# Differences of weight quarters written over the quarters themselves, and seven quarter products for the keys and values of a cross-attention

## The chip, the cores and the metric

The kernel runs on one core of a Trainium2 chip. The time is that of the whole kernel on the device, in microseconds (us). A single profiled execution gives the trace; its span runs from the first to the last instruction.

## The reference, cut to what matters

One layer works on `x` (256 tokens of 2048). The memory `mem` has 256 tokens of 2048 too. All is fp32. The parts that the change touches are the output projection behind the mixing stage and the memory's keys and values:

```python
h = h + jnp.concatenate([y_r, y_a], axis=-1) @ w_out[l]     # (256, 2048) @ (2048, 2048)
mem_n = rms_norm(mem, mem_norm[l])
k = (mem_n @ wk).reshape(B, M, XATT_HEADS, XATT_HEAD_DIM)    # (256, 2048) @ (2048, 512)
v = (mem_n @ wv).reshape(B, M, XATT_HEADS, XATT_HEAD_DIM)    # (256, 2048) @ (2048, 512)
s = jnp.einsum('bthd,bmhd->bhtm', q, k) * (XATT_HEAD_DIM ** -0.5)
```

Ahead of the projection stands an RWKV-7 recurrence over eight pairs of heads (`y_r`) beside a windowed attention (`y_a`). Behind the cross-attention stands a mixture of 32 experts, of which each has three matrices of 4 MB.

## The kernel before, in words

**Stages, in order of time.** The input projection runs to some 365 us. The recurrence then takes its eight pairs of heads one after the other, each some 26 us (the function `pair_`, once in the program of every engine). Then come the output projection in four blocks of 512 output columns, the memory's keys and values, the queries, scores and values of the cross-attention, the router, and the experts, from some 850 us to the end.

**Inside a pair.** TensorE runs 24 small steps (L1932 to L1967), each let go by a copy of ScalarE (L779, L781) and, for the last eight, by a sum that GpSimd makes with the identity (L539). VectorE meanwhile masks, scales and norms. At its start a pair adds an identity on GpSimd (L533) and sums keys (L536). What follows the 24 steps is L1973 to L2035 on TensorE, with VectorE at L1269 to L1287.

**A block of the output projection.** It is a product of 256 x 2048 by 2048 x 512, both cut in quarters: A11, A12, A21, A22 are 128 tokens by 1024, and B11, B12, B21, B22 are 1024 by 256. Seven products of sums of quarters replace eight of the quarters. Product number i stands in PSUM bank i; it is eight steps of 128 rows of the weights, and every fp32 step of 256 columns is two TensorE instructions in the trace. So a block has 56 steps, or 112 instructions (L2064). The sums of the left side (S1 to S4) are made during the recurrence by GpSimd (L544 to L549), those of the last head pair by VectorE (L1346 to L1351). The differences of the right side are T1 = B12 - B11, T2 = B22 - T1, T3 = B22 - B12 and T4 = B21 - T2, each one VectorE instruction of 128 x 2048. T1, T2 and T4 stand in the first 24 KB of `rest`, T3 over B12. Those of block 0 are made in the last pair (L1202 to L1218, called in `pair_` under `if last:`); those of block n + 1 are made while block n is multiplied.

VectorE collects the products with `w_op` and `w_add` (L1353 to L1366), 12 instructions in a block. Each of them waits for the one before it through the semaphore `op_add`, and for the product through `op_mm`.

**Between the last pair and block 0.** The last head pair's norm is still to be made: a mean on TensorE (L2056), the deviation and its square on VectorE (L1164, L1165), the variance on TensorE (L2076), the inverse root on ScalarE (L731, L733), and then VectorE to `gated` (L1181) and the last sums. The first 30 steps of block 0 (seven of product 1, eight of products 2 and 4, seven of product 5) need nothing of that result.

**Keys and values before.** `features` (L2111) makes keys turned over, features by tokens: four groups of 16 steps of 256 columns, 64 steps or 128 instructions. The values are 32 steps of 512 columns, 64 instructions (L2125). ScalarE copies each result out (L812, L815). `turn` (L1688) transposes a norm's rows on TensorE, 32 instructions; `turned` copies them back, half on VectorE and half on ScalarE.

**Weight loads.** The ring has three slots of 4 MB. `where` gives the slot of each load; SP issues each one when its slot's user before it has signalled `used`. Behind the values SP starts the experts' stream (`gate_up(0, "wg", 0)`), and from there each load waits for a step of TensorE.

## Time and profile before

| | us |
|---|---|
| median of three runs | 1792.4 (1790.73 to 1794.39) |
| the profiled execution | 1793.52 |
| its span | 1791.7 |
| TensorE matmul busy | 1692.2 (94%) |
| VectorE busy | 618.9 (35%) |
| ScalarE busy | 338.2 (19%) |
| GpSimd busy | 124.7 (7%) |

The profiled execution lies 1.1 us above the median, and its span 1.8 us under its own time. A timeline row gives the start, the duration of the whole merged group, the engine, the line and operation, the tiles, the number of instructions, and in brackets how long the engine had been idle and what ended that. The duration of a merged group runs from the first start to the last end; the next group may start before that end, since matmuls are pipelined. A source line can be that of a helper: all products stand at L2064, all collecting instructions at L1357. "issue" is a wait of an engine for which the profile shows no releaser.

### The profile page before, as it was taken

Reading aid. Unit: us, or ns where it says so; the run is one execution under the profiler, and the core shown is the slowest. Engines: PE = TensorE matmul, PEld = TensorE weight load, DVE = VectorE, ACT = ScalarE, POOL = GpSimd, SP = SyncE. Lnnn points to the kernel's source line nnn. Section 1 sums busy time; section 2 is a strip of 40 time slices with the busy share of each in tenths; the row PEclk is TensorE's granted clock in tenths of the full one; section 3 lists DMA queues with packets and bytes.
Section 4 is the critical chain, followed back from the end, with each engine's and each line's share of the span. In section 5 each row is a group of like instructions: output and inputs, shape, how many; then the busy total and the mean of one; then the engine's idle time right before and its main releaser. Section 6 shows DMA issues by size and latency. Waiting matters only on the chain.

```text
span 1791.7 us, 36478 instructions
## 1 busy us (share of the span) xinstructions
PE 1692.2 (94%) x15655; PEld 1123.0 (63%) x15655; DVE 618.9 (35%) x1330; ACT 338.2 (19%) x966; POOL 124.7 (7%) x206
## 2 busy tenths in 40 slices
PE   8999999989998999999999999999999999999996
PEld 7887888877777888576554554445444545454543
DVE  2001333488887462023123222232223222322233
ACT  2112222157666101122000000000000000000002
POOL 1000000013235000001000000000000000000000
PEclk9999999999999999999999999999999999999999
DMA  9932434300000944436999999999999999999995
GB/s 304 220 113 94 121 118 175 110 3 4 4 4 4 338 169 158 186 157 242 415 393 425 432 427 434 426 434 429 430 429 432 430 429 430 430 432 424 409 421 208
DMA packets 100783, 503.59 MB, mean 281 GB/s; under 512 B 38204, under 2 KB 42704, under 8 KB 81472
## 3 DMA queue, kind: packets, MB, share of 16 engines
q1 hardware_dynamic: 95960, 489.22, 68.2%
q0 software_dynamic: 4464, 12.03, 2.3%
q8 instruction: 94, 1.54, 0.4%
q10 hardware_dynamic: 248, 0.65, 0.1%
q14 instruction: 17, 0.14, 0.0%
HBM read 511.29 MB, written 4.23 MB: 288 GB/s over the span
## 4 chain that ended last, share of the span: by engine, by line
PE 70%; DMA 21%; DVE 4%; issue 2%; SPq 1%; ACT 1%; POOL 1%; DVEq 0%; ACTq 0%; POOLq 0%
PE ps L1734 15%; DMA rest<-in_wd 9%; DMA ring<-in_wu 9%; PE ps L2288 8%; PE ps L2280 8%; PE ps L2431 8%; PE ps L2064 5%; PE ps L2296 4%; DMA rest<-in_wu 2%; PE ps L2116 2%; PE ps L2167 2%; PE ps L2184 2%; PE ps L2125 2%; DMA ring<-in_wg 1%; PE ps L1951 1%
## 5 line engine op out<-in xcount | busy, mean ns | idle before, releaser
L1734 PE MATMUL ps<-wide,ring 128*128 128x256 f32 x1248 | 275.3, 379 | 1.2 <-PE ps L1734 0.9
L1734 PEld LDWEIGHTS ps<-wide,ring 128*128 128x128 f32 x1248 | 239.0, 195 | 39.7 <-issue 10.1
L2288 PE MATMUL ps<-ring,wide 128*64 128x256 f32 x1472 | 170.8, 391 | 28.9 <-DMA ring<-in_wu 28.7
L1594 DVE TENSOR_TENSOR tokA<-tokA,ps 128x512 f32<-128x512 f32 x256 | 158.5, 682 | 102.1 <-PE ps L2296 102.1
L2280 PE MATMUL ps<-ring,wide 128*64 128x256 f32 x1600 | 178.8, 381 | 2.9 <-DVE wide L1582 1.9
L1607 DVE SCALAR_TENSOR_TENSOR gg<-ps,tmp,gg 128x256 f32<-128x256 f32 x32 | 15.5, 484 | 472.4 <-PE ps L2288 472.4
L2431 PE MATMUL ps<-ring,gg 128*64 128x512 f32 x736 | 168.1, 598 | 0.8 <-DMA ring<-in_wd 0.8
L2288 PEld LDWEIGHTS ps<-ring,wide 128*64 128x64 f32 x1472 | 107.7, 141 | 91.3 <-DMA ring<-in_wu 36.9
L2280 PEld LDWEIGHTS ps<-ring,wide 128*64 128x64 f32 x1600 | 113.6, 137 | 60.2 <-DVE wide L1582 3.3
L2296 PE MATMUL ps<-wide,gg 64*128 64x512 f32 x512 | 135.3, 627 | 0.6 <-ACT wide L926 0.6
L2431 PEld LDWEIGHTS ps<-ring,gg 128*64 128x64 f32 x736 | 48.7, 136 | 114.5 <-issue 106.9
L918 ACT ACTIVATE wide<-ps 128x512 f32<-128x512 f32 x32 | 19.1, 598 | 449.7 <-PE ps L2431 449.7
L915 ACT ACTIVATE gg<-ps,tmp 128x256 f32<-128x256 f32 x32 | 15.2, 475 | 339.9 <-PE ps L2280 339.9
L570 POOL DMA_INDIRECT wide<-h_dram,sidx x17 | 17.1, 1008 | 889.9 <-DVE sidx L1546 889.1
L779 ACT ACTIVATE ring<-ps 128x384 f32<-128x384 f32 (+2 forms) x184 | 70.8, 421 | 27.9 <-PE ps L1954 7.5
L2296 PEld LDWEIGHTS ps<-wide,gg 64*128 64x128 f32 x512 | 41.5, 185 | 54.5 <-issue 50.2
L1013 DVE TENSOR_SCALAR tokA<-tmp,dprm 128x256 f32<-128x256 f32 x22 | 7.8, 354 | 192.3 <-ACT tmp L660 192.3
L2431 PE MATMUL ps<-rest,gg 128*64 128x512 f32 x288 | 65.5, 598 | 3.4 <-DMA rest<-in_wd 2.3
L2288 PE MATMUL ps<-rest,wide 128*64 128x256 f32 x528 | 58.8, 379 | 1.8 <-DMA rest<-in_wu 1.8
L2288 PEld LDWEIGHTS ps<-rest,wide 128*64 128x64 f32 x528 | 37.7, 137 | 21.6 <-DMA rest<-in_wu 3.0
L2280 PE MATMUL ps<-rest,wide 128*64 128x256 f32 x448 | 49.9, 381 | 0.0
L2431 PEld LDWEIGHTS ps<-rest,gg 128*64 128x64 f32 x288 | 19.8, 136 | 46.2 <-issue 39.2
(381 smaller groups left out, 2203.7 us busy)
## 6 DMA issues: line engine op xcount, KB each, us to landing
ring<-in_wu SPq DMA_DIRECT2D x20, 4096.0 KB, 29.5
ring<-in_wg SPq DMA_DIRECT2D x19, 4096.0 KB, 28.4
ring<-in_wd SPq DMA_DIRECT2D x19, 4096.0 KB, 30.8
rest<-in_wd SPq DMA_DIRECT2D x8, 4096.0 KB
ring<-in_w_in SPq DMA_DIRECT2D x7, 4096.0 KB, 16.4
rest<-in_wg SPq DMA_DIRECT2D x6, 4096.0 KB
rest<-in_wu SPq DMA_DIRECT2D x6, 4096.0 KB
ring<-in_w_out SPq DMA_DIRECT2D x4, 4096.0 KB, 19.5
```

Source lines behind the costliest of these rows:

```text
L779: ins = A(PRN[(l + 1) % 2][:, g, :, k], got[:, :, k], ACT.Copy)
L1594: V.tensor_tensor(fin_part(t, h, n), fin_part(t, h, n), ps[:, banks[q][h], :], ALU.add).then_inc(S["added"], 1)
L1734: ins = mm(ps[0:rows_, m % 2, 0:T], lhs, hnT[:, k, :], start=k == 0, stop=k == KD - 1)
L2064: ins = mm(ps[:, i, 0:T], lhs[:, k], rhs[:, k], start=k == 0, stop=k == CT - 1)
L2116: ins = mm(ps[:, f, 0:T], slot_k(s)[:, k, P * f:P * f + P], x[:, k, :], start=k == 0, stop=k == KD - 1)
L2125: ins = mm(ps[:, 4 + b, :], memT[:, k, P * b:P * b + P], slot_k(where[L_V])[:, k, :], start=k == 0, stop=k == KD - 1)
L2167: ins = mm(ps[:, f % 2, 0:T], slot_k(where[L_Q])[:, k, P * f:P * f + P], hnT[:, k, :], start=k == 0, stop=k == KD - 1)
L2184: ins = mm(ps[:, WO_BANK[n], :], oT[:, h, P * b:P * b + P], slot_d(where[L_O])[:, h, q], start=h == 0, stop=h == XH - 1)
L2280: ins = mm(ps[CAP * h:CAP * h + CAP, 0, 0:T], xT[:, k, CAP * i:CAP * i + CAP], in_k(p)[:, k, T * h:T * h + T], start=k == 0, stop=k == KD - 1)
L2288: ins = mm(ps[CAP * h:CAP * h + CAP, 1, 0:T], xT[:, k, CAP * i:CAP * i + CAP], w[:, T * h:T * h + T], start=k == 0, stop=k == KD - 1)
L2296: ins = mm(ps[:, banks[q][h], :], OHT[rows_, i, P * t:P * t + P], ysb[rows_, F * n:F * n + F], start=True, stop=True)
L2431: ins = mm(ps[CAP * h:CAP * h + CAP, 4 + n, :], half(hgT, k), in_d(dn)[:, k, o:o + F], start=k == 0, stop=k == 3)
```

## The change

The differences now stand in the quarters' own places: T1 over B11, T3 over B12, T2 over B22, T4 over B21. Each can be written only when the product of the quarter under it has been made, so they are made inside their own block; the products run in the order 1, 2, 3, 5, 7, 6, 4 (block 0: 2, 1, 3, 5, 7, 6, 4). None is made in the last pair. In block 0, T1 comes in two pieces, seven eighths behind the first seven steps of product 1 and one eighth behind its last. There the variance's matmul stands behind two steps of product 2; the steps ahead of the last pair's result are 22.

Keys and values become blocks 4 and 5 of the same kind, with the quarters of the turned memory on the left. Four sums of 128 x 1024 (M_S1 to M_S4) are made on VectorE behind the memory's turn. The collecting instructions are 8 in each of the two. Keys now come out tokens by features, so eight transposes on TensorE and two copies on ScalarE turn them, between products of the values. The norm of the cross-attention's rows (`normed(2)`) moves behind the keys' differences on VectorE.

```diff
@@ -207,8 +207,11 @@
-        W_T1, W_T2, W_T4 = (rest[:, CT * T * n:CT * T * n + CT * T].rearrange("p (k n) -> p k n", n=T) for n in range(3))
         W_U = tmp[:, 1280:1536]
+        M_A11, M_S3, M_A12, M_A22 = memT[:, 0:CT, 0:P], memT[:, 0:CT, P:T], memT[:, CT:KD, 0:P], memT[:, CT:KD, P:T]
+        M_S1, M_S2 = (rest[:, 24 * T + C * n:24 * T + C * n + C].rearrange("p (k t) -> p k t", t=P) for n in range(2))
+        M_S4 = oT[:].rearrange("p h t -> p (h t)").rearrange("p (k t) -> p k t", t=P)
+        krow = tmp[:, 0:1024].rearrange("p (b n) -> p b n", b=2)
...
@@ -282,6 +285,7 @@
+        W_BASE = (0, 12, 24, 36, 48, 56, 64)
...
@@ -807,15 +811,12 @@
             std(2, 3, "sq_done", 6)
-            for f in range(4):
-                act.wait_ge(S["xk_mm"], f + 1)
-                A(kxT[:, f, :], ps[:, f, 0:T], ACT.Copy).then_inc(S["xk_ev"], 1)
-            for b in range(TB):
-                act.wait_ge(S["xk_mm"], 5 + b)
-                A(vx[:, b, :], ps[:, 4 + b, :], ACT.Copy).then_inc(S["xk_ev"], 1)
+            for n in range(2):
+                act.wait_ge(S["xk_mm"], n + 1)
+                A(kxT[:, 2 * n:2 * n + 2, :].rearrange("p f t -> p (f t)"), ps[:, 0, :], ACT.Copy).then_inc(S["xk_ev"], 1)
...
-                    dve.wait_ge(S["op_mm"], 7 * (n - 1) + 4)
-                V.tensor_tensor(W_T1, W_B12(n), W_B11(n), ALU.subtract).then_inc(S["w_t"], 1)
...
-                V.tensor_tensor(W_T2, W_B22(n), W_T1, ALU.subtract).then_inc(S["w_t"], 1)
+            def w_t1(n, k=slice(0, CT)):
+
+                ins = V.tensor_tensor(W_B11(n)[:, k], W_B12(n)[:, k], W_B11(n)[:, k], ALU.subtract)
+                if k.stop == CT:
+                    ins.then_inc(S["w_t"], 1)
 
             def w_t3(n):
                 dve.wait_ge(*later("w_t", 4 * n + 1))
                 V.tensor_tensor(W_B12(n), W_B22(n), W_B12(n), ALU.subtract).then_inc(S["w_t"], 1)
 
+            def w_t2(n):
+                dve.wait_ge(*later("w_t", 4 * n + 2))
+                V.tensor_tensor(W_B22(n), W_B22(n), W_B11(n), ALU.subtract).then_inc(S["w_t"], 1)
+
...
+                dve.wait_ge(*later("w_t", 4 * n + 3))
+                V.tensor_tensor(W_B21(n), W_B21(n), W_B22(n), ALU.subtract).then_inc(S["w_t"], 1)
...
-                if last:
-                    w_t1(0)
-                    w_t2(0)
...
-                if last:
-                    w_t3(0)
-                    w_t4(0)
...
+            def made(n, count):
+                dve.wait_ge(S["op_mm"], 7 * n + count)
+
             w_ops = [0]
             dve.wait_ge(S["x2_in"], 16)
             for n in range(4):
+                dve.wait_ge(landed[where[L_OUT + n]], arrived[L_OUT + n])
                 if n == 0:
-                    dve.wait_ge(S["op_mm"], 1)
+                    made(n, 1)
                     w_add(n, 0, 0, product(2))
-                    dve.wait_ge(S["op_mm"], 2)
-                    w_add(n, 1, 0, product(4))
-                    dve.wait_ge(S["op_mm"], 3)
+                    dve.wait_ge(*later("w_p1", 1))
+                    w_t1(n, slice(0, CT - 1))
+                    made(n, 2)
                     w_op(W_U, product(1), None)
                     w_add(n, 0, 0, W_U)
...
+                    w_t1(n, slice(CT - 1, CT))
+                else:
+                    made(n, 1)
+                    w_op(W_U, product(1), None)
+                    w_add(n, 0, 0, W_U)
+                    w_t1(n)
+                    made(n, 2)
+                    w_add(n, 0, 0, product(2))
+                w_t3(n)
+                made(n, 3)
+                w_add(n, 0, 1, product(3))
+                w_t2(n)
+                w_t4(n)
+                made(n, 4)
+                w_add(n, 0, 1, product(5))
+                w_add(n, 1, 1, product(5))
+                made(n, 6)
...
+                made(n, 7)
                 w_add(n, 1, 0, product(4))
...
+            dve.wait_ge(S["hn_tr"], 16)
+            dve.wait_ge(S["hn_ev_a"], 8)
+            dve.wait_ge(S["hn_ev_v"], 8)
+            V.tensor_tensor(M_S1, M_S3, M_A22, ALU.add).then_inc(S["w_s7"], 1)
+            dve.wait_ge(*later("w_s7", 5))
+            V.tensor_tensor(M_S2, M_S1, M_A11, ALU.subtract).then_inc(S["w_s7"], 1)
+            dve.wait_ge(*later("w_s7", 6))
+            V.tensor_tensor(M_S4, M_A12, M_S2, ALU.subtract).then_inc(S["w_s7"], 1)
+            V.tensor_tensor(M_S3, M_A11, M_S3, ALU.subtract).then_inc(S["w_s7"], 1)
+
+            def memory_block(n, rows_):
+
+                lo, hi = slice(0, T), slice(T, 2 * T)
+                dve.wait_ge(landed[where[L_OUT + n]], arrived[L_OUT + n])
+                made(n, 1)
+                w_op(W_U, product(1), None)
+                w_t1(n)
+                made(n, 2)
+                w_op(rows_[:, 0, lo], W_U, product(2))
+                w_t3(n)
+                made(n, 3)
+                w_t2(n)
+                w_t4(n)
+                if n == 4:
+                    normed(2)
+                made(n, 6)
+                w_op(W_U, W_U, product(6))
+                w_op(rows_[:, 0, hi], W_U, product(5))
+                w_op(rows_[:, 0, hi], rows_[:, 0, hi], product(3))
+                w_op(W_U, W_U, product(7))
+                w_op(rows_[:, 1, hi], W_U, product(5))
+                made(n, 7)
+                w_op(rows_[:, 1, lo], W_U, product(4))
+
+            memory_block(4, krow)
+            memory_block(5, vx)
...
-            def product(n, i, lhs, rhs, ks=range(CT)):
-
-                if n >= 1 and ks[0] == 0:
-                    pe.wait_ge(S["op_add"], W_EACH * (n - 1) + (W_READ if n >= 2 else W_READ0)[i])
+            def product(n, i, lhs, rhs, ks=range(CT), ends=True):
...
-
-            W_READ0 = {2: 1, 4: 2, 1: 3, 5: 6, 6: 7, 3: 9, 7: 10}
-            W_READ = {1: 1, 2: 3, 6: 4, 5: 7, 7: 8, 3: 11, 4: 12}
+                return ins
+
+            W_READ0 = {2: 1, 1: 2, 3: 4, 5: 6, 6: 7, 7: 9, 4: 12}
+            W_READ = {1: 1, 2: 3, 3: 4, 5: 6, 6: 7, 7: 9, 4: 12}
+            M_READ = {1: 1, 2: 2, 6: 3, 3: 5, 7: 6, 5: 7, 4: 8}
             first, final = range(CT - 1), range(CT - 1, CT)
+
+            def combined_products(n, s1, s2, s3, a22):
+                pe.wait_ge(*later("w_t", 4 * n + 1))
+                product(n, 5, s1, W_B11(n))
+                pe.wait_ge(*later("w_t", 4 * n + 2))
+                product(n, 7, s3, W_B12(n))
+                pe.wait_ge(*later("w_t", 4 * n + 3))
+                product(n, 6, s2, W_B22(n))
+                pe.wait_ge(*later("w_t", 4 * n + 4))
+                product(n, 4, a22, W_B21(n))
+                pe.wait_ge(S["op_mm"], 7 * n + 7)
+                pe.sem_inc(used[where[L_OUT + n]], 1)
+
             landing(L_OUT)
-            pe.wait_ge(*later("w_t", 4))
-            pe.wait_ge(*later("w_s", 2 * (CT - 1)))
-            product(0, 1, W_A11, W_B11(0), first)
+            product(0, 2, W_A12, W_B21(0), range(0, 2))
             pe.wait_ge(S["rw_dsq"], CT)
             mm(ps[:, 7, T:2 * T], ones2, DSQ, start=True, stop=True).then_inc(S["rw_var"], 1)
-            product(0, 2, W_A12, W_B21(0))
-            product(0, 4, W_A22, W_T4)
-            product(0, 5, W_S1, W_T1, first)
+            product(0, 2, W_A12, W_B21(0), range(2, CT))
+            pe.wait_ge(*later("w_s", 2 * (CT - 1)))
+            product(0, 1, W_A11, W_B11(0), first).then_inc(S["w_p1"], 1)
+            product(0, 3, W_S4, W_B22(0), first)
             pe.wait_ge(S["rw_out"], CT)
             product(0, 1, W_A11, W_B11(0), final)
             pe.wait_ge(*later("w_s7", 4))
-            product(0, 5, W_S1, W_T1, final)
-            product(0, 6, W_S2, W_T2)
-            product(0, 3, W_S4, W_B22(0))
-            product(0, 7, W_S3, W_B12(0))
-            pe.wait_ge(S["op_mm"], 7)
-            pe.sem_inc(used[where[L_OUT]], 1)
+            product(0, 3, W_S4, W_B22(0), final)
+            combined_products(0, W_S1, W_S2, W_S3, W_A22)
             for n in range(1, 4):
                 landing(L_OUT + n)
                 product(n, 1, W_A11, W_B11(n))
                 product(n, 2, W_A12, W_B21(n))
-                pe.wait_ge(*later("w_t", 4 * n + 2))
-                product(n, 6, W_S2, W_T2)
-                product(n, 5, W_S1, W_T1)
-                pe.wait_ge(*later("w_t", 4 * n + 3))
-                product(n, 7, W_S3, W_B12(n))
                 product(n, 3, W_S4, W_B22(n))
-                pe.wait_ge(*later("w_t", 4 * n + 4))
-                product(n, 4, W_A22, W_T4)
-                pe.wait_ge(S["op_mm"], 7 * n + 7)
-                pe.sem_inc(used[where[L_OUT + n]], 1)
+                combined_products(n, W_S1, W_S2, W_S3, W_A22)
...
-            def features(n, x, count):
-                landing(n)
-                s = where[n]
-                for f in range(4):
-                    for k in range(KD):
-                        ins = mm(ps[:, f, 0:T], slot_k(s)[:, k, P * f:P * f + P], x[:, k, :], start=k == 0, stop=k == KD - 1)
-                    ins.then_inc(S["xk_mm"], 1)
-                pe.wait_ge(S["xk_mm"], count)
...
-            features(L_K, memT, 4)
+            def keys_turned(n):
+                for f in (2 * n, 2 * n + 1):
+                    for b in range(TB):
+                        o = T * (f % 2) + P * b
+                        ins = tr(ps[:, 0, o:o + P], krow[:, b, P * f:P * f + P], ident)
+                ins.then_inc(S["xk_mm"], 1)
+
+            landing(L_K)
+            product(4, 1, M_A11, W_B11(4))
+            product(4, 2, M_A12, W_B21(4))
+            pe.wait_ge(*later("w_s7", 8))
+            product(4, 3, M_S4, W_B22(4))
+            combined_products(4, M_S1, M_S2, M_S3, M_A22)
             landing(L_V)
-            for b in range(TB):
-                for k in range(KD):
-                    ins = mm(ps[:, 4 + b, :], memT[:, k, P * b:P * b + P], slot_k(where[L_V])[:, k, :], start=k == 0, stop=k == KD - 1)
-                ins.then_inc(S["xk_mm"], 1)
-            pe.wait_ge(S["xk_mm"], 6)
-            pe.sem_inc(used[where[L_V]], 1)
-            pe.wait_ge(S["xk_ev"], 6)
+            product(5, 1, M_A11, W_B11(5))
+            product(5, 2, M_A12, W_B21(5))
+            pe.wait_ge(S["op_add"], W_BASE[5])
+            keys_turned(0)
+            product(5, 3, M_S4, W_B22(5))
+            pe.wait_ge(S["xk_ev"], 1)
+            keys_turned(1)
+            combined_products(5, M_S1, M_S2, M_S3, M_A22)
+            pe.wait_ge(S["xk_ev"], 2)
+            pe.wait_ge(S["op_add"], W_BASE[6])
             pe.wait_ge(S["hn_done"], 3)
```

## Rows read from the trace of the kernel before

**Rows 1.** Chain of waits that ended last, shares of the span by engine, from the page.

```profile
PE 70%; DMA 21%; DVE 4%; issue 2%; SPq 1%; ACT 1%; POOL 1%; DVEq 0%; ACTq 0%; POOLq 0%
```

**Rows 2.** Busy time by stretch: us, each engine's busy us (instructions), TensorE's clock, DMA, GB/s.

```profile
579.80:584.70 4.90, 4.86 (x88) 3.58 (x89) 0.01 (x1) 2.93 (x10) 2.72 (x7) 0.65 0.02 3
...
590.50:616.10 25.60, 25.30 (x116) 21.96 (x116) 10.47 (x21) 5.35 (x8) 0.00 (x0) 1.00 1.03 397
...
1100.00:1791.00 691.00, 639.07 (x4346) 326.78 (x4342) 191.47 (x348) 58.31 (x156) 11.00 (x11) 0.99 0.97 414
```

**Rows 3.** Timeline (start, us, engine, line, idle before) of the last pair, several engines.

```profile
574.54 2.50 DVE L1212 TENSOR_TENSOR ring<-ring 128x2048 f32<-128x2048 f32 x1
...
575.13 0.44 PE L1964 MATMUL ps<-cst_sb,ring 128*128 128x128 f32 x2
...
575.60 5.23 POOL L539 TENSOR_TENSOR ring<-ring,cst_sb 128x128 f32<-128x128 f32 x5 [0.71 <-ACT ring L779]
...
576.96 2.50 DVE L1218 TENSOR_TENSOR rest<-ring,rest 128x2048 f32<-128x2048 f32 x1
...
579.78 1.21 PE L1957 MATMUL ps<-ring 64*64 64x64 f32 x24 [1.96 <-POOL ring L539]
...
584.69 0.29 DVE L1269 TENSOR_TENSOR ring<-ring,ps 128x128 f32<-128x128 f32 x1 [5.24 <-PE ps L1986]
```

**Rows 4.** Timeline of the same part of the pair before the last.

```profile
547.91 2.57 POOL L539 TENSOR_TENSOR ring<-ring,cst_sb 128x128 f32<-128x128 f32 x5 [7.63 <-ACT ring L779]
...
548.86 0.44 PE L1964 MATMUL ps<-cst_sb,ring 128*128 128x128 f32 x2
...
552.39 0.60 PE L1967 MATMUL ps<-tokA,cst_sb 128*128 128x256 f32 x2
...
552.92 0.34 PE L1957 MATMUL ps<-ring 64*64 64x64 f32 x8
...
555.12 0.29 DVE L1269 TENSOR_TENSOR ring<-ring,ps 128x128 f32<-128x128 f32 x1 [0.71 <-PE ps L1986]
```

**Rows 5.** Chain of waits in the last pair: start, us, what.

```profile
573.76 0.86 issue
```

**Rows 6.** Timeline from the end of the last pair into the first block, TensorE and VectorE.

```profile
590.53 0.70 PE L2056 MATMUL ps<-tmp,cst_sb 128*128 128x256 f32 x2 [0.94 <-DVE tmp L1287]
...
591.73 0.42 DVE L1165 TENSOR_TENSOR tmp<-tmp 128x256 f32<-128x256 f32 x1
...
594.09 0.59 PE L2076 MATMUL ps<-tmp,cst_sb 128*128 128x256 f32 x2
...
598.65 0.28 DVE L1351 TENSOR_TENSOR wide<-wide 128x128 f32<-128x128 f32 x1
```

**Rows 7.** Timeline at the end of the fourth block and the start of the turn.

```profile
686.37 3.62 PE L2064 MATMUL ps<-rest,wide 128*128 128x256 f32 x16
...
690.02 0.42 DVE L1357 TENSOR_TENSOR tokA<-tokA,ps 128x256 f32<-128x256 f32 x1 [3.03 <-PE ps L2064]
...
690.50 3.71 PE L1688 MATMUL ps<-cst_sb,rest 128*128 128x128 f32 x32 [0.52 <-DVE tokA L1357]
```

**Rows 8.** Groups by line and shape, 590 to 700 us: count, busy us, mean ns.

```profile
L1357 DVE TENSOR_TENSOR tokA<-tokA,ps 128x256 f32<-128x256 f32 x20 | 8.4, 420 | 21.4 <-PE ps L2064 21.1
...
L1212 DVE TENSOR_TENSOR ring<-ring 128x2048 f32<-128x2048 f32 x3 | 6.9, 2284 | 0.0
```

**Rows 9.** Timeline of the memory's keys and values and of the turn behind them.

```profile
695.14 27.89 PE L2116 MATMUL ps<-rest,ring 128*128 128x256 f32 x128 [0.93 <-ACT rest L642]
...
723.19 27.70 PE L2125 MATMUL ps<-ring,rest 128*128 128x512 f32 x64
...
751.58 3.71 PE L1688 MATMUL ps<-cst_sb,wide 128*128 128x128 f32 x32 [0.69 <-ACT rest L815]
```

**Rows 10.** Timeline of the DMA queue of SP: the expert stream's first load.

```profile
751.01 0.35 SPq L378 DMA_DIRECT2D ring<-in_wg  x1
```

**Rows 11.** Chain of waits, longest pieces: its first long wait for a weight load.

```profile
1101.49 30.15 DMA rest<-in_wu
```

More of the change, by code:

```diff
@@ L1196, in mask @@
                                 ps[:, 2 * g:2 * g + 2, 0:T].rearrange("p e (i n) -> p e i n", i=2), mk, ALU.mult).then_inc(S["rw_mask"], 1)
-            def w_t1(n):
-                dve.wait_ge(landed[where[L_OUT + n]], arrived[L_OUT + n])
-                if n >= 1:
-                    dve.wait_ge(S["op_mm"], 7 * (n - 1) + 4)
-                V.tensor_tensor(W_T1, W_B12(n), W_B11(n), ALU.subtract).then_inc(S["w_t"], 1)
-            def w_t2(n):
-                if n >= 1:
-                    dve.wait_ge(S["op_mm"], 7 * (n - 1) + (5 if n == 1 else 3))
-                dve.wait_ge(*later("w_t", 4 * n + 1))
-                V.tensor_tensor(W_T2, W_B22(n), W_T1, ALU.subtract).then_inc(S["w_t"], 1)
+            def w_t1(n, k=slice(0, CT)):
+                ins = V.tensor_tensor(W_B11(n)[:, k], W_B12(n)[:, k], W_B11(n)[:, k], ALU.subtract)
+                if k.stop == CT:
+                    ins.then_inc(S["w_t"], 1)
             def w_t3(n):
@@ L1212, in w_t3 @@
                 V.tensor_tensor(W_B12(n), W_B22(n), W_B12(n), ALU.subtract).then_inc(S["w_t"], 1)
+            def w_t2(n):
+                dve.wait_ge(*later("w_t", 4 * n + 2))
+                V.tensor_tensor(W_B22(n), W_B22(n), W_B11(n), ALU.subtract).then_inc(S["w_t"], 1)
             def w_t4(n):
-                if n >= 1:
-                    dve.wait_ge(S["op_mm"], 7 * (n - 1) + (2 if n == 1 else 7))
-                dve.wait_ge(*later("w_t", 4 * n + 2))
-                V.tensor_tensor(W_T4, W_B21(n), W_T2, ALU.subtract).then_inc(S["w_t"], 1)
+                dve.wait_ge(*later("w_t", 4 * n + 3))
+                V.tensor_tensor(W_B21(n), W_B21(n), W_B22(n), ALU.subtract).then_inc(S["w_t"], 1)
             def pair_(p, first, last, next_):
@@ L1377, in _ @@
                     w_op(W_U, product(1), None)
                     w_add(n, 0, 0, W_U)
-                    dve.wait_ge(S["op_mm"], 4)
-                    w_add(n, 0, 1, product(5))
-                    w_add(n, 1, 1, product(5))
-                    w_t1(n + 1)
-                    dve.wait_ge(S["op_mm"], 5)
-                    w_op(W_U, W_U, product(6))
-                    w_add(n, 0, 1, W_U)
-                    w_t2(n + 1)
-                    w_t3(n + 1)
-                    dve.wait_ge(S["op_mm"], 6)
@@ L1389, in _ @@
-                    w_add(n, 0, 1, product(3))
-                    dve.wait_ge(S["op_mm"], 7)
-                    w_op(W_U, W_U, product(7))
-                    w_add(n, 1, 0, W_U)
-                    w_add(n, 1, 1, W_U)
-                    w_t4(n + 1)
-                    continue
-                dve.wait_ge(S["op_mm"], 7 * n + 1)
-                w_op(W_U, product(1), None)
-                w_add(n, 0, 0, W_U)
-                dve.wait_ge(S["op_mm"], 7 * n + 2)
-                w_add(n, 0, 0, product(2))
@@ L1412, in _ @@
                 w_add(n, 1, 1, W_U)
-                if n < 3:
-                    w_t2(n + 1)
-                    w_t3(n + 1)
-                dve.wait_ge(S["op_mm"], 7 * n + 6)
-                w_add(n, 0, 1, product(3))
-                dve.wait_ge(S["op_mm"], 7 * n + 7)
+                made(n, 7)
                 w_add(n, 1, 0, product(4))
-                if n < 3:
-                    w_t4(n + 1)
                 if n == 1:
@@ L1424, in _ @@
             turned(1)
-            normed(2)
+            dve.wait_ge(S["hn_tr"], 16)
[31 more added lines that the diff above has]
+            memory_block(5, vx)
             turned(2)
@@ L2135, in scored @@
             def scored(h):
-                pe.wait_ge(S["xk_ev"], 7 + h)
+                pe.wait_ge(S["xk_ev"], 3 + h)
                 if h >= 2:
@@ L2174, in _ @@
                     valued(f - 3)
-            pe.wait_ge(S["xk_mm"], 10)
+            pe.wait_ge(S["xk_mm"], 6)
             pe.sem_inc(used[where[L_Q]], 1)
```

18 lines of the change are left out of this document (6 added, 12 removed).

## The prediction

> **What bounds the kernel now.** First the chain of waits from the page: TensorE carries 70% of it, weight loads 21%, VectorE 4% [rows 1]. Then the chain in order of time: its first long wait for a weight load comes at 1101 us [rows 11]. Ahead of that the end is set by TensorE and by who holds it up; behind it the DMA engines are busy for 97% of the time [rows 2]. All that the change touches lies between 565 and 752 us, in TensorE's part. The SP queue starts the experts' stream only at 751.01, when the values have let their slot go [rows 10], and each later load waits for a step of TensorE. So I take it that what TensorE gains before 751 moves the stream and the end with it, one for one.
>
> Last the timelines, for what each engine waits for. Three places count: the last pair, the start of block 0, and the keys and values.
>
> **The last pair: differences removed.** T3 and T4 of block 0 run on VectorE at 574.54 and 576.96, 2.5 us each. Beside them GpSimd takes 5.23 us for five small sums, and TensorE waits 1.96 us for one of them [rows 3]. In the pair before, the same five take 2.57 us [rows 4]. TensorE leaves that wait at a lower clock: 0.65 granted from 579.8 to 584.7, a mixture of 2.4 and 1.2 GHz [rows 2]. So the price is best read over the whole stretch. From the first transposes at L1964 to VectorE's first sum at L1269 the last pair needs 584.69 - 575.13 = 9.56 us [rows 3]. The pair before needs 555.12 - 548.86 = 6.26, of which 552.92 - 552.39 = 0.53 is the matmul at L1967, which the last pair hasn't [rows 4]; that leaves 5.73. **Gain: 9.56 - 5.73 = 3.8 us.** Lower bound: the wait that is seen, 1.96 [rows 3]. Upper bound: 3.8 and the 0.86 of "issue" just ahead [rows 5], 4.7, should that go too; nothing in the change speaks to it, and I leave it in. T1 and T2 lie beside GpSimd's key sums, which are wanted only behind the 24 steps, so I give their removal nothing.
>
> The Trainium skill, SBUF — State Buffer, section "SBUF: two separate sides", has a rule that bears on this: VectorE and GpSimd share a pair of ports, and a VectorE instruction with two SBUF inputs holds it whole while a GpSimd instruction that reads SBUF waits. The trace agrees: one wait of 1.96 us beside an instruction of 2.5 [rows 3]. By the rule alone only GpSimd's excess would come back, 5.23 - 2.57 = 2.7 us, and the forecast would be 1.1 us later.
>
> **The start of block 0.** A step of a product costs TensorE two instructions at (3.62 - 0.38) / 15 = 0.216 us, so 0.432 [rows 7]. From a product's last instruction to VectorE's start I take 690.02 - (686.37 + 16 x 0.216) = 0.19 us [rows 7]. I work in the clock of the old trace, without the shift from the pair.
> - The first product starts at 594.09 - 7 x 0.432 = 591.07 [rows 6]. Two steps on, at 591.93, the variance's matmul could go, but the squares are ready only at 591.73 + 0.42 = 592.15 [rows 6]: it goes at 592.2, a wait of 0.27, and 1.9 us earlier than now. The last sums of VectorE then end at 598.65 + 0.28 - 1.9 = 597.0 [rows 6].
> - TensorE goes on at 592.63 with 6 + 7 + 7 steps to 601.27, and two single steps to 602.13. Before, 30 steps stood here, and TensorE never waited.
> - VectorE needs 2.28 us for a difference of 2048 columns and 0.42 for 256 columns [rows 8], so some 2.0 for 1792. T1's long part starts when seven steps of product 1 are made, 592.63 + 13 x 0.432 + 0.19 = 598.4, and ends at 600.5. Product 1 is whole at 601.70 + 0.19 = 601.9; a copy, an add (0.42 each and a little between) and T1's rest then end at 603.1. Product 5 starts at 603.15.
> - New wait: 603.15 - 602.13 = 1.0 us. **Cost: 1.0 + 0.27 = 1.3 us.** Bounds: 0.3, if the collecting overlaps fully, and 2.5, if T1 cost in place by a half more.
> What is queued behind VectorE's waits in this block is only more collecting; nobody but TensorE waits for it.
>
> **The other differences, inside their blocks.** Nothing is added to VectorE's work, it is moved: 4 x 2.28 + 12 x 0.46 = 14.6 us in a block of 24.7. From a block's start: product 1 is there at 3.6, T1 at 6.9, wanted at 10.4; T3 at 9.8, wanted at 13.8; product 3 at 10.6, T2 at 13.3, wanted at 17.3; T4 at 15.6, wanted at 20.7. The shortest slack is 3.5 us, so **0** for blocks 1 to 3. One difference is already written in place, T3 over B12, at 2284 ns [rows 8]; the others should cost that. The last collecting instruction is still the add of product 4, so the turn starts as now, 0.06 behind it [rows 7]. `normed(1)` fits between blocks 1 and 2.
>
> **Keys and values.** Now keys take 723.19 - 695.14 = 28.05 us, of which 0.40 is handing over, and values 751.58 - 723.19 = 28.39, of which 0.9 is the end of the last matmul and ScalarE's copy [rows 9]. After:
> - Keys: 112 x 0.216 + 0.40 = 24.6.
> - Values: 24.2, eight transposes at (3.71 - 0.27) / 31 = 0.11 each [rows 9], 0.9, and at the end 0.19 + 0.42 + 0.06 for the last add, 0.7: 25.8.
> - **Gain: 56.4 - 50.4 = 6.0 us.**
> What must stay hidden: the four sums of 128 x 1024. Between the two durations of [rows 8], each is some 1.22 us, together 4.9 us from 695.1; product 3 wants them 6.9 us in. T1 of the keys then ends 8.0 us in, wanted at 10.4; T4 and `normed(2)` behind it end some 18.5 in, before product 6 is made at 20.9. The trace shows no such chain, so the bounds are 6.9 (no transposes in the way) and, if every sum waited in the open, 6.0 - 4.9 = 1.1. I take 6.0, since each link has a row. ScalarE's two copies of keys lie under products of 3.5 us. The rows' norm on VectorE is moved back by some 12 us and its turn is due 30 us later.
>
> **Sum.** -3.8 + 1.3 - 6.0 = -8.5 us. Against the profiled execution: 1793.5 - 8.5 = 1785.0, span 1783.2. That execution lay 1.1 above the median, so the median goes from 1792.4 to **1783.9**.
>
> **The rivals.**
> 1. *GpSimd is not freed* (0.12): something else holds the last pair, as code loading, of which the 0.86 of "issue" would be a part [rows 5]. Then the pair gives 0, and the sum is 1.3 - 6.0 = -4.7: 1787.7. Against it: the five sums are slow only in that pair [rows 3, 4].
> 2. *The clock falls at the new wait* (0.06). After 1.96 us of waiting the stretch behind ran at 0.65 for 4.9 us, which costs 4.9 x 0.35 = 1.7 us; after 0.94 us at 590.5 it stayed at 1.00 [rows 2, 3, 6]. The new wait is 1.0. If it fell: 1785.6. The Trainium skill, TensorE: Matmul & The Clock Gate, section "What's actually happening", says that the clock follows how busy TensorE has been of late; by that both rows fit, and the new wait is an open case.
> 3. *The memory's sums come into the open* (0.09): VectorE's chain behind the memory's turn is late, and the keys and values lose what they gain. -3.8 + 1.3 = -2.5: 1789.9.
> 4. *The loads swallow it* (0.08): the stream behind 1101 is bound by bytes, and if the transfers at 751 to 850 already ran against each other, an earlier start would bring little: some 1792. Against it: TensorE, not a load, carries the chain there [rows 11].
> 5. *Differences in place are dear* (0.05), the slow end. If VectorE took t for each when it writes what it reads, then from t = 3.9 us on T4 comes late by 4t - 15.7 in each of six blocks; from 4.3 us that eats the 8.5. At twice the row, 4.56: 6 x 2.5 + 1 = 16 lost, so 1792.4 - 8.5 + 16 = 1799.9. Against it: T3's row [rows 8].
>
> **How the numbers follow.** The forecast's own case has 0.60; with the bounds of its terms it runs from 1792.4 - 4.7 + 0.3 - 6.9 = 1781.1 to 1788. For the range I add what two executions differ by at the lower end, 1780.5, and reach up to rival 3, 1790.0. Outside are rivals 4 and 5 and a little of the rest. A measurement of this kernel can tell some 0.2%, 3.6 us, from no change. Faster than 1788.8: the forecast's case, rivals 1 and 2, and a part of 3: 0.80. Within: most of 3, and 4: 0.15. Slower: 0.05.
>
> **What the new profile would show.** GpSimd's last five sums at L539 in some 2.5 us and TensorE's clock at 1.00 behind them; L1964 to L1269 in 5.7 us. One wait of TensorE of 1.0 us before product 5 of block 0, on VectorE, and none in blocks 1 to 3. Keys' first product to the rows' turn in 50.4 us, against 56.4. SP's first load of the experts some 8.5 us earlier, at 742.5. It would be wrong if TensorE waited for VectorE ahead of products 3, 5, 7, 6 or 4 anywhere else, or if that load came 8.5 us earlier and the end did not.

## The result and the profile after

The changed kernel takes **1805.2 us** (median of four runs, 1804.0 to 1807.1) against 1792.8 for the kernel before (four runs too): a ratio of 1.0071, with an interval of 1.0053 to 1.0088. Faster by 8.5 us was forecast, in a range of 1780.5 to 1790.0; it is slower by 12.4 and lies 15 us above the range. The profiled execution took 1805.6, its span is 1803.8.

The chain of waits of the changed kernel, shares of the span by engine, and behind it the line of the page for the queue that loads program code (queue and kind, packets, MB, share of the DMA engines):

```profile
PE 89%; issue 4%; DVE 4%; ACT 1%; DMA 0%; POOL 0%; DVEq 0%; ACTq 0%
...
q8 instruction: 139, 2.28, 0.5%
```

Before, weight loads had 21% of this chain [rows 1]; now they have none. TensorE has 89% of it, and 4% is "issue". The kernel before had 94 code packets on queue 8:

```profile
q8 instruction: 94, 1.54, 0.4%
```

Turn 1 and turn 2 are the two passes of `turn` ahead of and behind the keys and values. Up to turn 2 the trace goes as forecast. This is the last pair after (timeline: start, us, engine, line, tiles, idle before). Its first row, L1976, is the transpose that stood at L1964 before; L543 are GpSimd's sums, at L539 before:

```profile
576.56 0.44 PE L1976 MATMUL ps<-cst_sb,ring 128*128 128x128 f32 x2
...
577.02 0.41 POOL L543 TENSOR_TENSOR ring<-ring,cst_sb 128x128 f32<-128x128 f32 x1 [0.78 <-ACT ring L783]
577.76 0.41 POOL L543 TENSOR_TENSOR ring<-ring,cst_sb 128x128 f32<-128x128 f32 x1 [0.34 <-ACT ring L785]
578.52 1.15 POOL L543 TENSOR_TENSOR ring<-ring,cst_sb 128x128 f32<-128x128 f32 x3 [0.35 <-ACT ring L785]
...
578.99 0.71 PE L1969 MATMUL ps<-ring 64*64 64x64 f32 x16 [0.42 <-POOL ring L543]
...
582.20 0.29 DVE L1260 TENSOR_TENSOR ring<-ring,ps 128x128 f32<-128x128 f32 x1 [6.23 <-PE ps L1998]
```

GpSimd's five sums now take 579.67 - 577.02 = 2.65 us. TensorE waits 0.42 us for one of them, where it waited 1.96 before [rows 3]. From the first transpose to VectorE's first sum it is 582.20 - 576.56 = 5.64 us; it was 9.56, and 5.73 was forecast. In this stretch TensorE's clock is 1.00; before, 0.65 was granted behind the wait for GpSimd [rows 2] (columns: length; busy us of TensorE, its weight load, VectorE, ScalarE, GpSimd; clock; DMA; GB/s):

```profile
577.00:582.20 5.20, 4.76 (x137) 3.51 (x137) 0.00 (x1) 4.32 (x16) 3.67 (x9) 1.00 0.02 6
...
590.00:616.00 26.00, 24.82 (x114) 21.23 (x114) 17.04 (x26) 5.34 (x8) 0.00 (x0) 1.00 1.04 397
```

Block 0, TensorE and VectorE:

```profile
588.58 1.03 PE L2076 MATMUL ps<-ring,wide 128*128 128x256 f32 x4
...
599.51 0.42 DVE L1348 COPY tmp<-ps 128x256 f32<-128x256 f32 x1 [1.43 <-PE ps L2076]
599.97 0.42 DVE L1348 TENSOR_TENSOR tokA<-tokA,tmp 128x256 f32<-128x256 f32 x1
600.32 0.42 DVE L1201 TENSOR_TENSOR ring<-ring 128x256 f32<-128x256 f32 x1
...
600.79 3.72 PE L2076 MATMUL ps<-ring,wide 128*128 128x256 f32 x16 [0.88 <-DVE ring L1201]
```

The wait before product 5 is there, 0.88 us, behind a copy, an add and T1's last eighth. The clock stays at 1.00 through it (the second row of the fence above). Then the keys, the values, turn 2 and SP's first load of the experts:

```profile
689.53 3.71 PE L1700 MATMUL ps<-cst_sb,rest 128*128 128x128 f32 x32 [0.52 <-DVE tokA L1348]
694.17 6.09 PE L2076 MATMUL ps<-ring,rest 128*128 128x256 f32 x27 [0.93 <-ACT rest L646]
...
744.33 0.35 SPq L382 DMA_DIRECT2D ring<-in_wg  x1
...
744.76 1.50 PE L1700 MATMUL ps<-cst_sb,wide 128*128 128x128 f32 x12 [0.56 <-DVE rest L1348]
```

Keys and values take 744.76 - 694.17 = 50.59 us; before it was 751.58 - 695.14 = 56.44 [rows 9]. That is 5.85 us less, with 6.0 forecast. Turn 2 starts 6.8 us earlier, and SP's load 6.7 us earlier (751.01 before [rows 10]).

**So 6.8 us were in hand at turn 2, and the span still ends 12.1 us later.** All 18.9 us between lie in the experts. The waits of TensorE between 1000 and 1700 us, after and then before (for what, by whom: us in total, times, longest):

```profile
PE ps L2300 <- issue: 49.1, 10, 6.3
PE ps L2291 <- DVE wide L1594: 4.4, 12, 0.4
```

```profile
PE ps L2288 <- DMA ring<-in_wu: 27.2, 14, 3.3
PE ps L2271 <- DVE wide L1582: 4.4, 12, 0.4
```

Waits of 27.2 us for these weights are gone, and 49.1 us of "issue", in ten pieces, have come. They come at the head of the experts' loop, two in each of its five returns to its start. The chain of waits there, in order of time, and the timeline of TensorE at the next round of the loop:

```profile
1060.78 5.55 issue
1066.33 1.96 PE ps L2300 x6
1068.29 3.27 issue
1071.57 3.67 PE ps L2300 x15
```

```profile
1182.43 1.25 PE L2291 MATMUL ps<-cst_sb,wide 128*128 128x128 f32 x8 [0.37 <-DVE wide L1594]
1189.78 1.96 PE L2300 MATMUL ps<-ring,wide 128*64 128x256 f32 x6 [6.09 <-issue]
1195.87 4.39 PE L2300 MATMUL ps<-ring,wide 128*64 128x256 f32 x26 [4.13 <-issue]
```

At the same place of the kernel before there is no such wait:

```profile
1182.54 1.25 PE L2271 MATMUL ps<-cst_sb,wide 128*128 128x128 f32 x8 [0.36 <-DVE wide L1582]
1184.15 7.13 PE L2280 MATMUL ps<-ring,wide 128*64 128x256 f32 x64 [0.35 <-DVE wide L1582]
```

The last view names the suspect. In the DMA queues between 1050 and 1660 us the changed kernel has a line that the kernel before has not, queue 8 (packets, MB, share of the DMA engines; after first, then before):

```profile
q1 hardware_dynamic: 11152, 249.04, 95.8%
q8 instruction: 45, 0.74, 0.5%
```

```profile
q1 hardware_dynamic: 11975, 259.52, 99.3%
```

The packets on queue 8 are 16 KB each, and over the whole kernel one comes per 256 instructions of TensorE (94 in the kernel before, for some 24,030 instructions with the loop counted once). The experts' loop is 1605 instructions, 6.27 such pieces; it is gone through once and returns to its start five times. In the kernel before no round behind a return has a code load; in the changed kernel each has nine (139 - 94 = 45 over the whole kernel; of the 45 in the window one belongs to the first pass, and one comes behind 1660 us). This table is counted from TensorE's own records in the traces, good to about two instructions: the number ahead of the loop, divided by 256. A code load starts when TensorE has come to some part of a piece; the last one ahead of the first return starts at 0.71 to 0.86 of a piece in the ten traces. With one border per piece, put at 0.78, a loop of 6.27 crosses six borders or seven. The rows of the table alone put the border between 0.66, where the loop is reloaded, and 0.85, where it isn't.

```
kernel                      ahead of loop  in pieces  borders crossed  code loads 1050-1660
before                      20813          81.30      6                0
after                       20906          81.66      7                45
before + 23 tiny steps      +92            .66        7                44
after + 12 tiny steps       +48            .85        6                1
after + 41 tiny steps       +164           82.30      6                1
after - 9 small steps       -36            .53        6 or 7 (edge)    10
after + 64 tiny steps       21161          82.66      7                45
```

### The profile page after: what moved, and what is told of

Its sections match the earlier page's. It is cut to its first block, busy times and chain, and to the rows that moved or that the text cites. A ratio compares the mean times of both kernels' runs of the same rounds, so it can differ in the third digit from the quotient of the medians.

```text
span 1803.8 us, 36595 instructions
## 1 busy us (share of the span) xinstructions
PE 1691.1 (94%) x15695; PEld 1132.1 (63%) x15695; DVE 646.6 (36%) x1359; ACT 335.7 (19%) x962; POOL 116.5 (6%) x206
## 3 DMA queue, kind: packets, MB, share of 16 engines
q8 instruction: 139, 2.28, 0.5%
## 4 chain that ended last, share of the span: by engine, by line
PE 89%; issue 4%; DVE 4%; ACT 1%; DMA 0%; POOL 0%; DVEq 0%; ACTq 0%
PE ps L1746 15%; PE ps L2300 14%; PE ps L2451 13%; PE ps L2308 12%; PE ps L2076 8%; PE ps L2316 7%; PE ps L2187 2%; PE ps L2204 2%; PE ps L2291 1%; PE ps L1963 1%; PE ps L1958 1%; PE ps L1827 1%; DVE wide L1594 1%; PE ps L2426 1%; PE ps L1786 1%
## 5 line engine op out<-in xcount | busy, mean ns | idle before, releaser
L2300 PE MATMUL ps<-ring,wide 128*64 128x256 f32 x1600 | 196.1, 400 | 49.6 <-issue 49.1
L2300 PEld LDWEIGHTS ps<-ring,wide 128*64 128x64 f32 x1600 | 119.4, 144 | 118.4 <-issue 67.7
L2308 PE MATMUL ps<-ring,wide 128*64 128x256 f32 x1472 | 165.1, 379 | 0.0
L2308 PEld LDWEIGHTS ps<-ring,wide 128*64 128x64 f32 x1472 | 106.7, 137 | 54.6 <-issue 1.5
L2076 PE MATMUL ps<-ring,wide 128*128 128x256 f32 x320 | 71.1, 379 | 0.9 <-DVE ring L1201 0.9
L2076 PEld LDWEIGHTS ps<-ring,wide 128*128 128x128 f32 x320 | 60.7, 190 | 9.5 <-DVE ring L1201 1.3
## 6 DMA issues: line engine op xcount, KB each, us to landing
ring<-in_w_out SPq DMA_DIRECT2D x4, 4096.0 KB, 18.8
```

What stands on the lines that cost most here:

```text
L2076: ins = mm(ps[:, i, 0:T], lhs[:, k], rhs[:, k], start=k == 0, stop=k == CT - 1)
L2300: ins = mm(ps[CAP * h:CAP * h + CAP, 0, 0:T], xT[:, k, CAP * i:CAP * i + CAP], in_k(p)[:, k, T * h:T * h + T], start=k == 0, stop=k == KD - 1)
L2308: ins = mm(ps[CAP * h:CAP * h + CAP, 1, 0:T], xT[:, k, CAP * i:CAP * i + CAP], w[:, T * h:T * h + T], start=k == 0, stop=k == KD - 1)
```

## The experiments

The main theory, A: the change raised the count of instructions ahead of the loop by 93, that moved the loop against the 16 KB pieces, and the seventh border costs a reload in every round; all the rest went as forecast. "Tiny" steps are one-column matmuls into a free bank at TensorE's start (`TINY`), four instructions each; `SMALL` is a like knob ahead of the router's sums. Neither changes the work.

**The changed kernel, moved by 41 tiny steps.**

```diff
-TINY, SMALL = 0, 9
+TINY, SMALL = 41, 9
```

> The changed kernel with 41 one-column matmuls more at TensorE's very start, where it waits 8 us for the first tokens anyway (164 TensorE instructions). Theory A, layout of TensorE's program: the changed kernel loses in the experts' loop only because its TensorE program is 93 instructions longer ahead of the loop, so that the loop lies otherwise across the 16 KB pieces in which the program is loaded: 45 such loads stand between 1050 and 1660 us in its trace, none in that of before, and TensorE idles 5.4 us ('issue') at the start of each round. 164 + 93 = 257 instructions bring the loop back to before's place to within one instruction: no loads in the loop, the 5.4 us waits gone, about 1785 to 1787 us (1805.2 less the 18.8 us that the stretch from the first expert load to the end is longer). Rival B, the stage in front: the earlier start, the new contents of slots or the later norm disturb the experts' stream. Then the loads and waits stay and it stays near 1805.

Measured: 1784.8 us (1781.4 to 1786.8), ratio 0.9951, interval 0.9932 to 0.9970. The "issue" waits are gone and the weights carry the loop again:

```profile
PE ps L2308 <- DMA ring<-in_wu: 24.2, 10, 3.3
```

and queue 8 between 1050 and 1660 us:

```profile
q8 instruction: 1, 0.02, 0.0%
```

164 further instructions make the kernel 20 us faster; rival B, which had it stay near 1805, falls. What the forecast left out is the place of the loop, and with the loop at its old place the time is 0.9 us from the forecast.

**The kernel before, moved by 23.** The same knob on the kernel before: `TINY` 23 in place of 0.

> The kernel before with 23 one-column matmuls more at TensorE's start (92 instructions), nothing else. Theory A: its loop then lies where the changed kernel's does; 45 loads in the loop, a wait of some 5.4 us in each round, 1792.8 + 18.8 = 1811 to 1812 us. Rival B: the same computation in the same order with some 1 us more inside an idle stretch, so 1793.

Measured: 1812.9 us (1808.8 to 1814.6), ratio 1.0105, interval 1.0085 to 1.0125. TensorE's waits in this kernel:

```profile
PE ps L2280 <- issue: 49.8, 10, 6.9
```

Queue 8 has 44 packets between 1050 and 1660 us. The kernel before shows the same loss with none of the change in it; rival B (1793) falls. With the last run this gives four corners: loop at the old place, 1792.9 before and 1784.8 after; loop moved, 1812.9 before and 1805.2 after. By these medians the change is worth 8.1 us in one row and 7.7 in the other, and the place some 20 us in both. By the ratios it is 8.8 and 6.1 us for the change, 18.8 and 21.5 for the place; each ratio is known to some 3 or 4 us only.

**Two other places.** First `TINY` 12, which puts the loop past the border; then `SMALL` 0, which moves it back by 36 instructions.

> The changed kernel with 12 one-column matmuls more (48 instructions): the loop moves 48 of the 256 instructions of a piece on. Theory A: it is still in the bad part or just out of it, which bounds the part: near 1805 with loads in the loop, or near 1786 without; nothing between. A rival C, any lengthening costs in proportion: 1805 + a little.

> The changed kernel without the nine one-column matmuls that stand ahead of the router's sums (36 instructions less; they compute nothing that is used). Theory A: the loop moves 36 instructions back, which is not the 93 that would give before's place: near 1805 with loads in the loop, or near 1786 if the edge lies within those 36; nothing between. Rival B: 1805, less 0.7 us that they took.

Measured: 1786.6 us (ten runs, 1780.6 to 1791.6; ratio 0.9966, 0.9952 to 0.9980) and 1785.5 us (ten runs, 1781.9 to 1790.1; ratio 0.9965, 0.9952 to 0.9977). The first has one code load in the window, the first pass's own. The second, at the edge, has ten:

```profile
PE ps L2300 <- issue: 7.3, 2, 6.9
```

and queue 8 between 1050 and 1660 us:

```profile
q8 instruction: 10, 0.16, 0.1%
```

The first round was reloaded and the other four were not. So taking instructions away heals it as well as adding them. At 0.53 of a piece the loop ends at 0.80, close to the border by my count; why a single round is reloaded there, these runs don't tell. Both kernels lie near 1786, as theory A allowed; it had not said beforehand which side they would fall on. Rival C (1805 and a little) falls.

**A whole piece further: 64 tiny steps.** This tells the place within a piece from any effect of a later start or of a busier TensorE.

```diff
-TINY, SMALL = 0, 9
+TINY, SMALL = 64, 9
```

> The changed kernel with 64 one-column steps at TensorE's start, 256 instructions: one whole piece of code more, so the experts' loop starts at the same place of a piece as in the changed kernel (0.66). Theory A: the same waits in the loop and 1805 us, though the dose of 41 steps gave 1784.8. Rival D (any delay or any activity at TensorE's start cures it): 1784 to 1787, as with 12 and with 41 steps.

Measured: 1804.7 us (1803.5 to 1806.3), ratio 1.0063, interval 1.0048 to 1.0079, and again:

```profile
PE ps L2300 <- issue: 48.5, 10, 6.8
```

Queue 8 has 45 packets in the window. 12 and 41 steps heal, 64 don't. The time goes by the place modulo 256 instructions; rival D falls.

**The changed kernel with the old keys and values.** It computes them as the kernel before did, in 32 steps of 512 and 64 of 256 columns.

```diff
-TINY, SMALL = 0, 9
+TINY, SMALL = 53, 9
...
-            landing(L_K)
-            product(4, 1, M_A11, W_B11(4))
...
+            features(L_K, memT, 4)
+            landing(L_V)
+            for b in range(TB):
+                for k in range(KD):
+                    ins = mm(ps[:, 4 + b, :], memT[:, k, P * b:P * b + P], slot_k(where[L_V])[:, k, :], start=k == 0, stop=k == KD - 1)
```

> The changed kernel with the keys and values as before (192 TensorE instructions in place of 240, no sums of the memory's quarters), and 53 one-column steps at TensorE's start so that the experts' loop starts at the same place of a 256-instruction piece as before (0.30). If the seven products are worth 6.0 us at the end, as the sum had it and as turn 2 showed, this kernel takes 1784.8 + 6.0 = 1790.8, and the stage from turn 1 to turn 2 lasts 61.1 us. Rival (the stream of loads hides that stage): 1785 to 1787, though the stage is 5.9 us longer.

Measured: 1790.9 us (eleven runs, 1788.0 to 1792.3), ratio 0.9987, interval 0.9978 to 0.9996. The loop starts at 0.13 of a piece, not at the 0.30 that I meant, with six borders crossed and no code load in it. Turn 2 of this kernel and SP's first load:

```profile
747.26 0.35 SPq L382 DMA_DIRECT2D ring<-in_wg  x1
...
747.83 3.71 PE L1668 MATMUL ps<-cst_sb,wide 128*128 128x128 f32 x32 [0.69 <-ACT rest L819]
```

Turn 1 starts at 686.75, so from turn to turn it is 61.08 us against 55.23 in the changed kernel (744.76 - 689.53). The stage is 5.85 us longer and the end 6.1 us (1790.9 against 1784.8, on another chip; the kernel before took 1793.5 here and 1792.9 there). By the ratios of the two runs the end is 6.5 us later, known to some 4 us. The rival, 1785 to 1787, lies outside the runs of this kernel: the stream of loads hides nothing that they can resolve.

**The kernel before with T1 to T4 in eight pieces.** Each difference of block 0 becomes eight VectorE instructions of 256 columns. TensorE's program, and so the loop's place, is that of the kernel before.

```diff
-                V.tensor_tensor(W_T4, W_B21(n), W_T2, ALU.subtract).then_inc(S["w_t"], 1)
+                difference(n, W_T4, W_B21(n), W_T2)
...
+            def difference(n, out, a, b):
+                pieces = CT if n == 0 else 1
+                for k in range(pieces):
+                    o = slice(CT * k // pieces, CT * (k + 1) // pieces)
+                    ins = V.tensor_tensor(out[:, o], a[:, o], b[:, o], ALU.subtract)
+                ins.then_inc(S["w_t"], 1)
```

> The kernel before, with each of the four differences of the last pair cut into eight VectorE instructions over one eighth of the columns; TensorE's program is that of the kernel before to the instruction. Theory G (GpSimd's additions in the last pair last 5.23 us because each waits out a whole VectorE instruction of 2.5 us): with pieces of 0.3 us the additions beside L1212 and L1218 fall to 2.6 to 3.5 us, the last pair is 2 to 3.8 us shorter, and the time is 1789 to 1791. Rival V (VectorE's own 5 us ahead of its norm are what the last pair pays, whatever the length of an instruction): the last pair ends where it did, within 0.5 us, and the time stays at 1792.9 or goes up by 1 to 2 us for the 28 further instructions. In both the end follows the pair, since TensorE's first load signal moves with it.

Measured: 1791.6 us (eleven runs, 1788.1 to 1794.5), ratio 0.9990, interval 0.9981 to 0.9999. The last pair of this kernel:

```profile
576.63 3.64 DVE L1202 TENSOR_TENSOR ring<-ring 128x256 f32<-128x256 f32 x8
...
577.34 0.44 PE L1971 MATMUL ps<-cst_sb,ring 128*128 128x128 f32 x2
...
577.80 0.41 POOL L539 TENSOR_TENSOR ring<-ring,cst_sb 128x128 f32<-128x128 f32 x1 [0.83 <-ACT ring L779]
...
578.55 0.55 POOL L539 TENSOR_TENSOR ring<-ring,cst_sb 128x128 f32<-128x128 f32 x1 [0.34 <-ACT ring L781]
...
579.31 1.77 POOL L539 TENSOR_TENSOR ring<-ring,cst_sb 128x128 f32<-128x128 f32 x3 [0.21 <-ACT ring L781]
...
580.19 4.24 DVE L1202 TENSOR_TENSOR rest<-ring,rest 128x256 f32<-128x256 f32 x8
...
584.35 0.28 DVE L1276 TENSOR_TENSOR ring<-ring,ps 128x128 f32<-128x128 f32 x1
```

GpSimd's five sums take 581.08 - 577.80 = 3.28 us in place of 5.23, with more VectorE work beside them, not less (7.9 us for T3 and T4 in place of 5.0). The stretch from transpose to first sum is 7.01 us in place of 9.56. TensorE's clock is 1.00 there. So 2.55 of the 3.9 us come back by short instructions alone: theory G holds for these, and rival V, which had the pair end where it did, falls. The rest can't be told from this run, because VectorE itself is now late: its first sum follows T4's last piece with no idle time, where it had idled 5.24 us in the kernel before [rows 3]. The end moved by 1.9 us, less than the pair, and 1791.6 lies 0.6 above what theory G named; the interval of 0.2 to 3.4 us holds 2.55 too.

**The best version.** The changed kernel with 41 tiny steps and T1's last eighth ahead of the copy and the add:

```diff
                     made(n, 2)
+                    w_t1(n, slice(CT - 1, CT))
                     w_op(W_U, product(1), None)
                     w_add(n, 0, 0, W_U)
-                    w_t1(n, slice(CT - 1, CT))
```

> Theory A (layout of TensorE's program): the start of the experts' loop is where the 41-step dose put it, so no waits in the loop, and the time is that of the 41-step kernel, 1784.8, less what the swap of two VectorE steps in block 0 takes off: the last eighth of T1 now stands ahead of a copy and a sum of 0.42 us each, so TensorE's wait before product 5 (0.88 us in the changed kernel) should shrink to under 0.2, and the end come 0.7 us earlier, near 1784.1. Rival (that wait stands for something else than T1's last piece): the wait stays at 0.8 to 1.0 and the time at 1784.8.

Measured: **1782.9 us** (1780.6 to 1784.7), ratio 0.9944, interval 0.9931 to 0.9958. The wait is gone; product 3's last step and product 5 are one group of 18 instructions now:

```profile
597.40 4.40 PE L2076 MATMUL ps<-ring,wide 128*128 128x256 f32 x18
...
597.60 0.42 DVE L1201 TENSOR_TENSOR ring<-ring 128x256 f32<-128x256 f32 x1 [1.43 <-PE ps L2076]
```

From the mean's matmul to turn 1 it is 100.70 us (586.12 to 686.82), against 101.49 in the changed kernel (588.04 to 689.53): 0.8 us, the two VectorE steps that stood ahead. The gain is read from the trace; the difference of the medians, 1.9 us between two chips, is within the noise of the two ratios.

## Why the prediction was wrong

- **The last pair, -3.8: right.** Measured -3.9, with the clock at 1.00 and the 0.93 us of "issue" left in, as assumed. The pieces bear out the cause for 2.55 of it. By the rule of the Trainium skill, SBUF — State Buffer, section "SBUF: two separate sides", only GpSimd's excess of 2.7 us would come back; GpSimd's five sums came down by 5.23 - 2.65 = 2.6. But the pair gained 3.9; the other 1.3 us fit the lower clock behind the wait, which went too (4.9 us at 0.65 cost some 1.7 by rival 2's working), though no run sets it apart. The rows over the whole stretch were the better price.
- **Block 0, +1.3: right within 0.3.** From the mean's matmul to block 1 it is 27.1 us against 25.6, so +1.5. The wait before product 5 was put at 1.0; the profile calls 0.88 idle, and in the prediction's own measure (two instructions of 0.216 behind 599.32, to 600.79) it is 1.04. The clock did not fall there (rival 2).
- **Other differences, 0: right.** Blocks 1 to 3 last 24.71 us each, as before, with no wait of TensorE for VectorE ahead of a product. In place a difference takes 2.28 to 2.29 us; this is the group of T4, and one of the memory's sums (line, tiles, shapes, count, busy us, mean ns):

```profile
L1215 DVE TENSOR_TENSOR ring<-ring 128x2048 f32<-128x2048 f32 x4 | 9.2, 2292 | 0.1
...
L1405 DVE TENSOR_TENSOR rest<-rest 128x1024 f32<-128x1024 f32 x1 | 1.2, 1224 | 0.5 <-ACT rest L646 0.5
```

  So rivals 5 and 3 fall.
- **Keys and values, -6.0: right.** 5.85 in the trace, and about as much at the end when undone.
- **SP's first load, 742.5: 744.33.** The terms gave what they should; the last pair started 1.4 us later than before. In the ten kernels of this study, whose recurrence is the same but for the last pair, that start lies between 558.6 and 563.9 us in the profiled executions. I count the 1.4 us as such scatter and did not test it.
- **What TensorE gains moves the end one for one: the step that failed.** The prediction took it that the 8.5 us gained ahead of the stream move the end by as much; 6.8 us were gained at turn 2 and the end came 12.1 later. The rule itself holds where the loop stays at a harmless place: in the seven kernels with no round or one round reloaded, turn 2 to the end is 1037.3 to 1040.1 us (1037.8 with 41 steps, 1040.1 before). In the three with every round reloaded it is 1056.9 to 1059.0. What the step left out is that the change also alters how TensorE's program lies. The changed kernel has 1059.0 us, 21.3 more than the one with 41 steps, in three parts: 1.5 up to the loop, 23.8 in its five rounds (619.0 against 595.2), and 4.0 back behind it (125.3 against 129.3), where it has no wait for weights and the other has 3 us.
- **The 23.8 us of the rounds** are mostly idle time. These are the five rounds, in the changed kernel and in the one with 41 steps (start and end; columns as above):

```profile
1059.48:1678.47 618.99, 566.25 (x3821) 291.21 (x3822) 159.09 (x290) 43.29 (x120) 10.00 (x10) 0.95 0.97 414
```

```profile
1058.76:1654.02 595.26, 560.69 (x3821) 289.11 (x3822) 159.07 (x291) 43.29 (x120) 10.00 (x10) 0.99 1.00 430
```

  TensorE is idle for 52.7 us in place of 34.6, so 18.2 more, and the same 3821 matmuls keep it busy for 5.6 us longer, at a clock of 0.95 for 0.99. Most of the 49.1 us of "issue" takes the place of waits for weights (29.2 us with 41 steps); what exceeds them is lost. The clock falls behind the stops: it is 0.76 for 8 us there, a mixture of 2.4 and 1.2 GHz:

```profile
1072.00:1080.00 8.00, 8.00 (x60) 4.85 (x58) 0.00 (x0) 0.00 (x0) 0.00 (x0) 0.76 0.96 410
```

- **The rivals.** Rival 4 named the right stage, but by another mechanism, and at 1792 no loss. Rival 1 thought of code loading, but only for 0.86 us in the last pair. None of the five had the program's layout in the loop. The slow side got 0.05, by rival 5, whose price of 1799.9 is 5 us short of what came. The prediction's own sign of being wrong, a load that comes earlier and an end that doesn't, is what the trace shows. The page had the clue in its line for queue 8, 94 code packets of 16 KB, and I passed over it. Whoever adds or removes instructions of TensorE ahead of a loop of 6.27 pieces has to count: with one border per piece it crosses a seventh one from some 27% of all places, the 0.27 by which it exceeds six. That is an estimate from the length; seven places were measured. A chance of that size at +20 us should have been in the forecast.

With the place put right, the sum of the forecast holds within the noise: ratio 0.9951, which is -8.8 us of 1792.9 (interval -12.2 to -5.4), for -8.5 forecast. That the medians agree to 0.9 us is in part luck.

## What to carry to other kernels

A change that alters how many instructions TensorE runs ahead of a loop also moves the loop against the 16 KB pieces in which its code is loaded (other engines were not tried). Where the loop nearly fills what is held, compare both kernels at the same place, or pad, before judging the change. Look first at the code queue's packets within the loop: none, or nine in every round, told the good kernels from the bad ones here. Padding by some tens of one-column matmuls at TensorE's start, where it waits 8 us for its first data, cost nothing that these runs resolve. Short VectorE instructions beside GpSimd let it in between. A long one ahead of a small sum that TensorE waits for can cost more than the wait that is seen: here the wait was 1.96 us and the pair gained 3.9.

## What the runs showed of the hardware

TensorE's program comes in 16 KB pieces, one per 256 instructions. A loop of 1605 instructions that crosses six borders was never reloaded; the same loop across seven was reloaded whole, nine pieces, in every round, in three kernels. At the branch back of the changed kernel TensorE's matmuls stop for 6.1 to 6.3 us (5.4 to 5.6 of it behind the VectorE step that they had waited for), six run, and they stop for 3.3 to 4.1 us more. The branch instruction itself lasts 5.9 to 6.2 us in the trace, where it lasts 0.21 to 0.24 in the kernel before. In the first of these stops the last matmul ends at 1060.04 and the VectorE step that it waits for at 1060.78; the piece's transfer starts at 1063.12 and takes 1.1 us, and the first instruction of the new round follows at 1065.67. So most of the stop is not the transfer. The fast kernels have 94 or 95 packets in all, 103 with one round reloaded, and TensorE has no wait of "issue" in the loop where it is held. What the loads outside the loop cost was not measured.

The Trainium skill, Runtime: NRT & Kernel Launch, section "Instruction fetch mechanics", says that TensorE's instruction memory is 128 KiB, 2048 instructions, filled in blocks of 256, and that a taken branch whose target is not in the window forces a fetch. The trace agrees with the blocks and with the stop at the branch. The same section speaks of a window of two pages; here a loop that crosses six borders, and so by the count above lies on seven pieces, stayed without a load for five rounds, so for TensorE the measurement says otherwise. Nor did the page's 2048 instructions, eight pieces, hold the loop where by the same count it lies on eight.
